# Modulation vectors summed on VectorE instead of TensorE

## The reference, cut to what matters

```
ml = (silu(c)     @ ada_w[l] + ada_b[l]).reshape(B, N_MOD, 1, D)   # 1024 x 9216
mc = (silu(c_ctx) @ ada_w[l] + ada_b[l]).reshape(N_MOD, 1, 1, D)
x = x + 0.5*ml[:,2] * swiglu(modulate(rms(x, ffn1_norm), ml[:,0], ml[:,1]), ffn1_w_in, ffn1_w_out)
h = h + 0.5*mc[2]   * swiglu(modulate(rms(h, ffn1_norm), mc[0],   mc[1]),   ffn1_w_in, ffn1_w_out)
y_l = token_mix(modulate(rms(h, mix_norm), mc[3], mc[4]), modulate(rms(x, mix_norm), ml[:,3], ml[:,4]), ...)
x = x + ml[:,5] * y_l
x = x + 0.5*ml[:,8] * swiglu(modulate(rms(x, ffn2_norm), ml[:,6], ml[:,7]), ...)
```

## Time and profile before

| | before |
|---|---|
| median of 3 runs | 2487.57 us |
| lowest, highest | 2481.47, 2487.93 us |
| span of the profiled execution | 2484.4 us |
| PE, PEld busy | 97%, 81% |
| DVE, ACT busy | 58%, 47% |
| DMA | 161 GB/s mean |

### The profile page before, as it was taken

The page is one execution under the profiler, slowest core; times in us unless marked ns, Lnnn a source line. Parts: engine busy times, 40 slices in busy tenths (PEclk is TensorE's granted clock), DMA queues, the critical chain, the costliest instruction groups (busy, mean ns, idle before and its releaser), DMA issues.

```text
span 2484.4 us, 33336 instructions
## 1 busy us (share of the span) xinstructions
PE 2419.8 (97%) x13574; PEld 2011.8 (81%) x13574; DVE 1446.7 (58%) x2180; ACT 1170.6 (47%) x1730; POOL 13.1 (1%) x43
## 2 busy tenths in 40 slices
PE   7999999999999999999999999999999999999998
PEld 4777788888888887887888887788888888777887
DVE  3222232736756577666666468666666655767665
ACT  4211232525543345445545468554454446874444
POOL 0000000000000000000000000000000000000000
PEclk9999999999999999999999999999999999999999
DMA  8654222313431124554655534345545545334553
GB/s 327 238 223 183 86 101 100 138 51 136 153 135 69 68 102 146 190 195 170 215 187 187 216 136 152 119 170 187 187 170 193 194 177 211 125 114 177 187 186 136
DMA packets 57911, 399.66 MB, mean 161 GB/s; under 512 B 7785, under 2 KB 8305, under 8 KB 10272
## 3 DMA queue, kind: packets, MB, share of 16 engines
q1 hardware_dynamic: 52704, 383.80, 42.3%
q10 hardware_dynamic: 4264, 10.07, 1.2%
q0 software_dynamic: 800, 3.73, 0.5%
HBM read 396.52 MB, written 2.63 MB: 161 GB/s over the span
## 4 chain that ended last, share of the span: by engine, by line
PE 91%; DVE 4%; ACT 3%; DMA 1%; issue 1%; SPq 0%; DVEq 0%; ACTq 0%
PE pair L474 84%; DMA ring<-in_stream 1%; PE pair L805 1%; DVE ring_parts L2048 1%; PE pair L583 1%; PE pair L600 1%; PE pair L788 1%; PE pair L1178 1%; PE pair L941 1%; PE pair L1206 1%; PE pair L1192 0%; PE pair L1177 0%; DVE rows L2143 0%; DVE X L2149 0%; PE pair L752 0%
## 5 line engine op out<-in xcount | busy, mean ns | idle before, releaser
L474 PE MATMUL pair<-xT_parts,ring_high 128*128 128x512 f32 x2112 | 745.6, 395 | 3.1 <-DVE xT_parts L2030 3.1
L474 PE MATMUL pair<-xT_parts,ring_parts 128*128 128x256 f32 (+2 forms) x2448 | 694.9, 298 | 7.2 <-DVE ring_parts L2048 5.0
L2038 DVE TENSOR_TENSOR ring_parts<-ring,ring_high 128x2048 fp32r<-128x2048 f32 x198 | 453.5, 2292 | 159.5 <-ACT ring_high L1408 159.5
L474 PEld LDWEIGHTS pair<-xT_parts,ring_parts 128*128 128x128 f32 (+1 forms) x2448 | 461.5, 189 | 56.8 <-issue 18.3
L474 PEld LDWEIGHTS pair<-xT_parts,ring_high 128*128 128x128 f32 x2112 | 383.9, 188 | 79.1 <-issue 3.7
L1408 ACT ACTIVATE ring_high<-ring 128x2048 fp32r<-128x2048 f32 x198 | 378.1, 1911 | 97.1 <-DMA ring<-in_stream 97.0
L1453 ACT ACTIVATE arena<-pair 128x512 f32<-128x512 f32 x110 | 66.0, 600 | 308.9 <-PE pair L474 308.9
L2048 DVE TENSOR_TENSOR ring_parts<-ring,mix_high 128x1024 fp32r<-128x1024 f32 x144 | 167.4, 1219 | 50.0 <-ACT mix_high L1421 49.9
L474 PE MATMUL pair<-ring_parts,xT_parts 128*128 128x512 f32 (+1 forms) x448 | 176.0, 393 | 0.2 <-DVE rows L2256 0.2
L474 PE MATMUL pair<-mix_high,xT_parts 128*128 128x512 f32 (+1 forms) x576 | 171.9, 381 | 0.0
L474 PE MATMUL pair<-ring_parts,g_high 128*128 128x512 f32 x440 | 171.4, 389 | 0.0
(11 more groups left out here) (378 smaller groups left out, 3916.8 us busy)
## 6 DMA issues: line engine op xcount, KB each, us to landing
ring<-in_stream SPq DMA_DIRECT2D x338, 1024.0 KB, 4.8
xn<-in_mods SPq DMA_DIRECT2D x14, 1024.0 KB, 6.8
arena<-in_mods SPq DMA_DIRECT2D x14, 1024.0 KB, 9.1
arena<-in_bT ACTq DMA_DIRECT2D x1, 1536.0 KB, 10.2
bias_scratch<-bias_row POOLq DMA_DIRECT2D x1, 1536.0 KB, 7.7
X<-in_x ACTq DMA_DIRECT2D x1, 1024.0 KB, 11.9
X<-in_ctx ACTq DMA_DIRECT2D x1, 1024.0 KB, 16.4
arena<-in_bT ACTq DMA_DIRECT2D x1, 1024.0 KB, 8.1
```

What stands on the lines that cost most here:

```text
L474: m = pe.matmul(o, l, r, start=start, stop=stop)
L2038: dve.tensor_tensor(out=ring_r[:, slot].rearrange("p a b -> p (a b)"), in0=w, in1=high[:, slot, :], op=ALU.subtract).then_inc(low_ready, 1)
```

## The change

VectorE multiplies each row chunk of `ada_w` by silu(c) of its 128 rows (a scalar per partition) and adds it to a running sum of 128 x 512 per half vector and sequence (`mod_add`). TensorE then adds up the 128 partitions once per quad (`quad_sum`) with a stationary operand of one column of ones (`unit`; in the second of its two 32-column blocks the ones stand in the second column, so that the context's sum lands on the second row). Only what is used is summed: the context for quads 1 (3, 4) and for vector 2. The order of quads becomes (3, 4), (2, 5), (8), (6, 7). One modulation chunk is taken per up tile for f = 0..7 and two for f = 8..17. The rest of the diff follows from this: `scT` moves into `ones`, the running sums take free places in `gateB` and the arena, the last quad is turned in another PSUM bank, and two more small bias transfers are issued on ScalarE's queue.

```diff
-MODS = ((0, 1), (3, 4), (6, 7), (2, 5), (8,))
-MOD_TILES = 14
+MODS = ((0, 1), (3, 4), (2, 5), (8,), (6, 7))
+KEPT = {0: 0, 1: 1, 4: 2}
+MOD_STEPS = 18
+SUMMED_AT = {8: 1, 12: 2, 14: 3, 18: 4}
+TURNED_AT = {9: 1, 20: 4}
...
+        def mod_chunks(f):
+            return (f,) if f < KD else (2 * f - KD, 2 * f - KD + 1) if f < MOD_STEPS else ()
...
+        def sums_of(q):
+            if q == 3:
+                return [(0, 0, sum_x[1])]
+            if q == 4:
+                return [(0, i, sum_c[i]) for i in range(2)]
+            return [(0, i, sum_x[i]) for i in range(2)] + [(1, i, sum_c[i]) for i in range(2 if q == 1 else 1)]
...
                 f = n - QUAD - 3
-                if 0 <= f < MOD_TILES:
-                    for s in range(2):
-                        if f:
-                            sp.wait_ge(mod_read[s], f)
-                        sp.dma_start(mod_w[s], t["mods"][2 * f + s]).then_inc(mod_loaded[s], 16)
+                for m in mod_chunks(f) if f >= 0 else ():
+                    if m >= 2:
+                        sp.wait_ge(mod_added[m % 2], m // 2)
+                    sp.dma_start(mod_w[m % 2], t["mods"][m]).then_inc(mod_loaded[m % 2], 16)
...
+            def quad_sum(q):
+                pe.wait_ge(unit_set, 1)
+                pe.wait_ge(mod_added[1], {1: 4, 2: 8, 3: 10, 4: 14}[q])
+                if q >= 2:
+                    pe.wait_ge(mod_row, q - 1)
+                sums = sums_of(q)
+                for r, i, v in sums:
+                    for j in range(2):
+                        g = 2 * i + j
+                        mm(bank[4 + q % 2][32 * g:32 * g + 32, :], unit[:, 32 * r:32 * r + 32], v[:, j, :], r == 0,
+                           r == 1 or not any(s[:2] == (1, i) for s in sums),
+                           mod_full if (r, i) == sums[-1][:2] and j else None)
...
             def beside_up(f):
-                for s in range(2 if f < MOD_TILES else 0):
-                    n = 2 * f + s
-                    q, k = 1 + n // KD, n % KD
-                    if k == 0 and q >= 2:
-                        pe.wait_ge(mod_row, q - 1)
-                    pe.wait_ge(mod_loaded[s], 16 * (f + 1))
-                    if q < 4:
-                        quad_part(q, k, mod_w[s], mod_full if k == KD - 1 else None)
-                    else:
-                        quad_part(q, 2 * k, mod_w[s])
-                        quad_part(q, 2 * k + 1, mod_w[s][:, 2:4, :], mod_full if 2 * k + 1 == KD - 1 else None)
-                    owed.append(mod_read[s])
-                if f in (5, 9):
-                    quad_turn((f - 1) // 4)
+                if f in SUMMED_AT:
+                    quad_sum(SUMMED_AT[f])
+                if f in TURNED_AT:
+                    quad_turn(TURNED_AT[f])
...
+            def mod_add(m):
+                s = m % 2
+                q = 1 + m // KD if m < 2 * KD else 3 if m < 2 * KD + 4 else 4
+                dve.wait_ge(mod_loaded[s], 16 * (m // 2 + 1))
+                if m in (0, 8, 16, 20):
+                    dve.wait_ge(mod_full, q)
+                else:
+                    dve.wait_ge(mod_added[1 - s], (m - 1) // 2 + 1)
+                if q == 3:
+                    k = 2 * (m - 2 * KD)
+                    jobs = [(0, k, 0, sum_x[1]), (0, k + 1, 1, sum_x[1])]
+                else:
+                    jobs = [(r, (m - 4 if q == 4 else m) % KD, i, v) for r, i, v in sums_of(q)]
+                for r, k, i, v in jobs:
+                    w, by = mod_w[s][:, 2 * i:2 * i + 2, :], scT[:, k, r:r + 1]
+                    if k == 0:
+                        ins = dve.tensor_scalar(v, w, by, None, ALU.mult)
+                    else:
+                        ins = dve.scalar_tensor_tensor(out=v, in0=w, scalar=by, in1=v, op0=ALU.mult, op1=ALU.add)
+                    if q == 3 and i == 0:
+                        step(ins)
+                ins.then_inc(mod_added[s], 1)
...
             def beside_up(f):   # VectorE
-                if f in (4, 8, 12):
-                    quad_row(f // 4)
-                if f in (6, 10):
-                    quad_keep((f - 2) // 4)
-                if f == 14:
-                    quad_row(4)
+                if f in SUMMED_AT:
+                    quad_row(SUMMED_AT[f])
+                if f in TURNED_AT:
+                    quad_keep(TURNED_AT[f])
+                for m in mod_chunks(f):
+                    mod_add(m)
+                if f == MOD_STEPS - 1:
+                    dve.wait_ge(mod_added[1], 14)
```

More of the change, by code:

```diff
@@ L88, in build @@
         sil4 = room(FT * 2 * S + D, 2, N)
+        sum_x = [gateB[:, 2 * i + i, :].rearrange("p (a b) -> p a b", b=N) for i in range(2)]
+        sum_c = [room(FT * 2 * S, 2, N), room(25600, 2, N)]
         xTl = room(13312, KD, 2 * S)
@@ L156, in build @@
         ones = sb("ones", [P, S])
+        scT = ones[:, :].rearrange("p (a b) -> p a b", b=32)
+        unit = gcol[:, :, :].rearrange("p a b -> p (a b)")[:, 0:64]
         ssq = sb("ssq", [P, 16])
@@ L278, in build @@
         mod_loaded = [sem(f"modulation_chunk_loaded{i}") for i in range(2)]
-        mod_read = [sem(f"modulation_chunk_read{i}") for i in range(2)]
+        mod_added = [sem(f"modulation_chunk_added{i}") for i in range(2)]
+        unit_set = sem("unit_columns_set")
         mod_full = sem("modulation_products")
@@ L436, in ffn_order, with turn_bank @@
             return order + [("down", FT // 2 - 2), ("down", FT // 2 - 1)]
+        def mod_chunks(f):
[6 more added lines that the diff above has]
+            return [(0, i, sum_x[i]) for i in range(2)] + [(1, i, sum_c[i]) for i in range(2 if q == 1 else 1)]
+        def turn_bank(q):
+            return bank[5 if q == 4 else 6]
         def norm_bank(t_, h):
@@ L449, in _ @@
                 sp.dma_start(ring[:, j], t["stream"][j]).then_inc(loaded[j], 16)
-            turns, whole = NCH // SLOTS, (QUAD + MOD_TILES + 2) // SLOTS + 1
+            turns, whole = NCH // SLOTS, (QUAD + MOD_STEPS + 2) // SLOTS + 1
             for n in range(SLOTS, SLOTS * whole):
@@ L524, in quad_turn @@
                 if q:
-                    pe.wait_ge(mod_kept, q)
+                    pe.wait_ge(mod_kept, KEPT[q])
                 picked = ident[:, :].rearrange("p (a b) -> p a b", b=32)[:, :, 0:2]
                 for j in range(4):
-                    mm(bank[6][:, 8 * j:8 * j + 8], modrow[:, q % 2, j * P:(j + 1) * P], picked, True, True,
+                    mm(turn_bank(q)[:, 8 * j:8 * j + 8], modrow[:, q % 2, j * P:(j + 1) * P], picked, True, True,
                        mod_turned if j == 3 else None)
@@ L535, in gate_row @@
                 if n == 0:
-                    pe.wait_ge(mod_kept, 3)
+                    pe.wait_ge(mod_kept, 2)
                     pe.wait_ge(late_consts, LATE_CONSTS)
@@ L1333, in modulation @@
                     act.dma_start(gateB[rows_, 1:3, :], t["adab"][2 * g:2 * g + 2, 0:4 * N]).then_inc(more_consts, 16)
-                for g in range(2):
+                for g in range(4):
                     act.dma_start(tmp[32 * g:32 * g + 2, 0, :], t["adab"][2 * g:2 * g + 2, 4 * N:5 * N]).then_inc(
@@ L1964, in quad_keep @@
             def quad_keep(q):
[L1966 to L1970, removed]
+                z = KEPT[q]
+                dve.wait_ge(mod_turned, z + 1)
+                dve.tensor_copy(modT[:, 16 * z:16 * z + 16, :].rearrange("p (g j) r -> p g j r", j=4),
+                                turn_bank(q)[:, 0:32].rearrange("p (j g r) -> p g j r", j=4, r=2)).then_inc(mod_kept, 1)
@@ L1971, in quad_keep @@
+                dve.wait_ge(mod_kept, z + 1)
+                for r in range(2 if z < 2 else 1):
                     c.mod += 1
-                    dve.scalar_tensor_tensor(out=normA[:, 2 * q + r, :], in0=modT[:, 16 * q + 8:16 * q + 16, r],
-                                             scalar=1.0, in1=gains[:, q, :], op0=ALU.add,
+                    dve.scalar_tensor_tensor(out=normA[:, 2 * z + r, :], in0=modT[:, 16 * z + 8:16 * z + 16, r],
+                                             scalar=1.0, in1=gains[:, z, :], op0=ALU.add,
@@ L1980, in modulation @@
                 dve.memset(tmp[:, 0, :], 0.0).then_inc(zeroed, 1)
+                dve.memset(unit[:, 0:1], 1.0)
+                dve.memset(unit[:, 1:33], 0.0)
+                dve.memset(unit[:, 33:34], 1.0)
+                dve.memset(unit[:, 34:64], 0.0).then_inc(unit_set, 1)
             def modulation_ready():
@@ L1992, in beside_up @@
                     lower_bounds()
-                if f in (4, 8, 12):
-                    quad_row(f // 4)
-                if f in (6, 10):
-                    quad_keep((f - 2) // 4)
-                if f == 14:
-                    quad_row(4)
+                if f == 0:
+                    dve.wait_ge(sc_done, 1)
+                if f in SUMMED_AT:
[6 more added lines that the diff above has]
+                    dve.wait_ge(mod_added[1], 14)
             def first_vars(nt):
@@ L2873 @@
 MORE_CONSTS = 16 * 5
-LATE_CONSTS = 16 * 6
```

(5 more changed lines are left out.)

1 line of the change is left out of this document (removed).

## The result

| | before | after |
|---|---|---|
| median in the comparison | 2486.50 us | 2461.35 us |
| all runs | 2481.47 to 2487.93 | 2455.18, 2461.06, 2461.63, 2462.23 |
| span of the profiled execution | 2484.4 us | 2453.5 us |
| PE, PEld, DVE busy | 2419.8, 2011.8, 1446.7 us | 2386.6, 1999.1, 1538.5 us |

The ratio is 0.9898, 95% interval 0.9883 to 0.9913: the kernel is about 1.0% faster, 25 us. A second comparison, with five rounds, gave 0.9887 (0.9871 to 0.9904). The profiled execution is the fastest of its four, and its device time is 2455.18 us, 1.7 above its span. One execution of one variant (e1_pe_off) took 10930.08 us instead of about 2462 and is left out of that variant's ratio.

The account below looks back on a forecast made before the run. TensorE was taken as the bound: 32.7 us removed, less 6.7 for new sums, 0.4 for turns and 2.0 for a wait, saves 23.6; span 2484.4 - 23.6 = 2460.8, plus 3.2 gives 2464.0 us, range 2457 to 2470.

Parts of the forecast that it names:

- TensorE's blocks are on the path at full length, 32.7 us: In the first layer's up tiles, the modulation matmuls lengthen the strides between silus; removing them takes 32.7 us off.
- The phase: The stretch from silu 0 to silu 21 of the up tiles: 268.12 us before, forecast about 244.5 us.
- The third rival: In the up tiles, TensorE was not the bound: removed time becomes idle and the time stays 2487.6 us; chance 0.03.
- Quad 4's rounds fill only two column groups and cost as much as full ones: Behind up tiles 12 and 13, quad 4's old matmuls cost 3.78 and 3.56 us, against 2.12 for other blocks.
- The new sums, 6.7 us: TensorE's sums after tiles 8, 12, 14 and 18: 2.12 us each for quads 1 and 2, 1.24 for 3 and 4.
- Turns alone, 1.1 each: Turns in the up tiles no longer stand behind a block: 1.1 us each instead of 0.91, 0.4 us more.
- VectorE free of charge but for one wait of 2.0 us: VectorE's 80 operations, 102 us, fit its gaps; TensorE waits only at the second quad's sum, behind tile 12, 2.0 us.
- the allowance of 0.4 for handovers: At the second quad's sum, handovers from chunk to chunk raised the wait from 1.6 to 2.0 us.
- The sum: All terms together, in the up tiles: 23.6 us saved, span 2460.8 us, median 2464.0 us.
- Later stages unchanged: Nothing behind the first layer's up tiles changes, and no transfer there is timed by anything but the ring.
- the second rival: Behind the wait at the second quad's sum, the clock falls to 1.2 GHz; up to 1.8 us, 2466; chance 0.08.
- Late chunks: Modulation chunks of f = 10 and 11 land late, TensorE waits 5.1 us at the second quad's sum; 2468; chance 0.12.

Follow-up runs that it names:

- e1_pe_off: Kernel before, with TensorE's modulation matmuls of quads 1 to 4 issued only for each quad's last row chunk; 2462.36 us, ratio 0.9899.
- e8_four_groups: Kernel before, with quad 4's matmuls spread over all four column groups, the two halves of the sum not added; 2481.87 us, ratio 0.9985.
- e7_sums_twice: Changed kernel with every one of TensorE's sums over the partitions issued twice; 2466.16 us, ratio 0.9915.
- e4_load_after_add: Changed kernel, with each modulation chunk requested only when the chunk before it has been added; 2494.34 us, ratio 1.0035.
- e3_dve_double: Changed kernel with every multiply-and-add issued twice, each waiting for the one before it; 2512.39 us, ratio 1.0110.

## Why the prediction was right

- *TensorE's blocks are on the path at full length, 32.7 us.* Right. The phase shows it, and leaving the matmuls out (e1_pe_off) gives back 24.6 of 27.7 us, the rest having turned into waits. The third rival rested on the headroom that the Trainium skill reads from the busy share of weight loads ("Perfetto Trace Analysis", Identifying the Most-Contended Engine). PEld is busy for 81% of the span in both kernels: that share told nothing of what removing matmuls gives, and the strides did. (Two silus in the rows had been idle for 3.65 and 6.47 us and not for 7 to 13, as the prediction has it; this changes nothing.)
- *Quad 4's rounds fill only two column groups and cost as much as full ones.* Right: e8_four_groups returned 3.4 us.
- *The new sums, 6.7 us.* Measured 2.12 + 2.12 + 1.21 + 1.23 = 6.68, and e7_sums_twice doubled them by 5.2 where 5.3 was expected.
- *Turns alone, 1.1 each.* Measured 11.83 - 10.88 = 0.95.
- *VectorE free of charge but for one wait of 2.0 us.* Right in place and kind, too high in size: 1.37. The estimate of 1.28 us an operation took the record's length, but two in a row overlap by 0.08 us. So the six of f = 11 took 7.46 us instead of 7.68 and ended 1.22 us after silu 12 instead of 1.52; and of the allowance of 0.4 for handovers 0.1 was needed at the end (186.97 to 187.06). The size of 1.28 came out (1280 ns), though the 58 ns in it came from two rows that differ in more than the scalar: L2509 also reads one operand from PSUM. And the first operation of a sum, a plain multiply, was priced like the others and takes about 0.75 us (L2021); with the overlap this makes 92 us of VectorE's time instead of 102. None of these ten stands where TensorE waits.
- *The sum.* 228.5 + 5.1 + 1.9 + 6.7 + 1.4 = 243.6 us for the phase; forecast 244.5, measured 243.55. Saved 24.6, forecast 23.6. The median came at 2461.35 against 2464.0: 1.0 us of that is this, 1.1 the median of before, which fell from 2487.57 to 2486.50 with more runs, the rest lies in the clock's spread. The part that was worked out, the phase, was off by 1.0 us.
- *Later stages unchanged.* In work yes, in time no: 6.6 us, which the granted clock accounts for. The prediction used that effect only for the wait, and for the range it used the spread of the runs of before, which is where it belongs. The passage of the Trainium skill that the second rival names ("TensorE: Matmul & The Clock Gate") stands there under "What's actually happening": the default state is throttled, and activity releases it. The trace agrees in kind: after 20.6 us without a matmul the granted clock was 0.51 from 206 to 212 us (e4_load_after_add), and at 236.79 us a block took 1.05 us again.
- *Late chunks.* Did not happen: VectorE never waits for a modulation chunk in the changed kernel, and where two are used per tile each lands after 4.7 to 4.9 us. There they are mostly requested alone; with a ring chunk 0.4 us ahead they take 6.7 to 8.3, and in the kernel before, with three requests within 1.3 us, 6.8 and 9.1. That the number of requests makes the difference fits all three, but no run changes it alone. e4_load_after_add shows what chunks that come late cost.

## What to carry to other kernels

When one engine sets the pace and another has gaps, moving work pays by what leaves the path, but the price on the other engine must be worked out tile by tile: here four operations a tile fit, six did not, and the deficit appeared only where TensorE asked for the result. Put the collecting step one tile behind the deficit. Read strides of a repeating marker instead of busy shares, and compare the phase that was changed, since the whole kernel's time carries 6 us of clock changes that the edit did not make.

## What the hardware showed that was not expected

- A float32 matmul with a stationary operand of 32 columns, four of them on different column groups, takes 0.86 to 0.88 us for the four; two on two groups take the same 0.87.
- A multiply-and-add with a scalar per partition takes 1280 ns at 1024 elements; the nearest form with a constant takes 1220 (L2639, which reads one tensor twice and has another second operation, so the 60 ns need not be the scalar's alone). Queued ones follow each other every 1.20 us, and every 1.26 where each waits for the one before it (e3_dve_double).
- TensorE waited for 1.35 us (changed kernel) and for 2.69 us (e4_load_after_add, at the third sum) and its next block ran at full speed, 1.07 and 1.05 us; behind waits of 6.04 us (e3_dve_double) and of 11.45 and 20.60 us (e4_load_after_add) it took 1.93 to 1.94 us. Behind a pause of 1.9 us in a later stage the clock of the changed kernel fell in one execution (0.91 from 415 to 435 us) and not in another (1.00). The program's executions take 2455 to 2456 or 2461 to 2462 us; that the same falls make this difference is read from the profiled executions of the variants.
